# Turning the attention weights and the head outputs of six heads on VectorE instead of TensorE

## What is computed

```python
def diff_attention(h, w_qkv, w_out, ...):      # 8 heads, two maps each, value width 256
    proj = h @ w_qkv
    # q, k: (S, 8, 2, 128), v: (S, 8, 256)
    logits = einsum('bqhcd,bkhcd->bhcqk', qb, k) * scale
    p = softmax(logits + bias, axis=-1)
    a = p[:, :, 0] - lam * p[:, :, 1]          # the attention weights
    o = einsum('bhqk,bkhe->bqhe', a, v)
    o = rmsnorm(o, subln_g) * (1 - lambda_init) # the normed head output
    return o.reshape(B, S, 8 * 256) @ w_out
```

## Time and profile before

| | us |
|---|---|
| median of 3 runs | 2162.86 (2162.79 to 2163.11) |
| span of the profiled execution, first to last instruction | 2161.1 |
| TensorE matmuls busy | 2152.5 |
| VectorE busy | 1394.3 |
| ScalarE busy | 1020.2 |
| GpSimd busy | 15.1 |

### The profile page before, as it was taken

One profiled execution on the slowest core, in us unless ns is written; L12 is line 12 of the kernel. 1 busy time (PEld: TensorE's weight loads), 2 busy tenths in 40 slices (PEclk: granted clock), 3 DMA queues, 4 the chain that ended last, 5 costly groups with the idle time before them and its releaser, 6 DMA issues.

```text
span 2161.1 us, 30888 instructions
## 1 busy us (share of the span) xinstructions
PE 2152.5 (100%) x11158; PEld 1836.9 (85%) x11158; DVE 1394.3 (65%) x1951; ACT 1020.2 (47%) x1430; POOL 15.1 (1%) x28
## 2 busy tenths in 40 slices
PE   9999999999999999999999999999999999999998
PEld 8888888888888888888888888888888888888887
DVE  7777756755764665675577777657646656755754
ACT  6444445443543443454445445455434434434543
POOL 1000000000000000000000000000000000000000
PEclk9999999999999999999999999999999999999999
DMA  9644456555555555555555544545555555555553
GB/s 331 230 176 157 165 185 214 195 195 185 187 194 193 194 188 191 186 192 188 182 176 175 176 163 169 195 177 193 194 194 179 192 193 195 185 195 186 192 194 117
DMA packets 63567, 408.92 MB, mean 189 GB/s; under 512 B 6677, under 2 KB 12565, under 8 KB 15482
## 3 DMA queue, kind: packets, MB, share of 16 engines
q1 hardware_dynamic: 60304, 402.42, 52.2%
q10 hardware_dynamic: 2730, 3.55, 0.5%
q0 software_dynamic: 448, 1.77, 0.2%
HBM read 405.58 MB, written 2.14 MB: 189 GB/s over the span
## 4 chain that ended last, share of the span: by engine, by line
PE 99%; issue 0%; DVE 0%; POOL 0%; POOLq 0%; DVEq 0%; ACT 0%
PE acc L1093 32%; PE acc L1097 16%; PE ps_scores L1127 7%; PE ps_scores L1125 7%; PE ps_scores L1126 7%; PE ps_v L1125 4%; PE ps_v L1126 4%; PE ps_v L1127 4%; PE acc L1125 2%; PE acc L1126 2%; PE acc L1127 2%; PE ps_aux L1126 2%; PE ps_aux L1125 2%; PE ps_aux L1127 2%; PE ps_scores L1184 1%; PE ps_o L1184 1%
## 5 line engine op out<-in xcount | busy, mean ns | idle before, releaser
L666 DVE TENSOR_TENSOR w_lo<-raw,w_hi 128x1024 fp32r<-128x1024 f32 x744 | 908.6, 1223 | 513.9 <-ACT w_hi L362 511.4
L362 ACT ACTIVATE w_hi<-raw 128x1024 fp32r<-128x1024 f32 x744 | 787.4, 1059 | 632.4 <-PE ps_scores L1127 253.4
L1093 PE MATMUL acc<-gx,w_hi 128*128 128x512 f32 x3008 | 947.4, 396 | 0.0
L1097 PEld LDWEIGHTS acc<-gx,w_lo 128*128 128x128 f32 x3008 | 565.0, 188 | 133.4
L1097 PE MATMUL acc<-gx,w_lo 128*128 128x256 f32 x3008 | 591.5, 278 | 0.0
L1093 PEld LDWEIGHTS acc<-gx,w_hi 128*128 128x128 f32 x3008 | 460.3, 189 | 2.6 <-issue 0.5
L1125 PE MATMUL ps_scores<-w_hi,mid 128*128 128x512 f32 x640 | 249.5, 390 | 0.0
L1127 PE MATMUL ps_scores<-w_hi,mid 128*128 128x512 f32 x640 | 249.0, 389 | 0.0
L1126 PE MATMUL ps_scores<-w_lo,mid 128*128 128x512 f32 x640 | 249.0, 389 | 0.0
L369 ACT ACTIVATE copied<-acc 128x256 f32<-128x256 f32 x188 | 71.8, 382 | 317.4 <-PE acc L1097 317.4
L699 DVE TENSOR_TENSOR head<-acc,copied 128x256 f32<-128x256 f32 x188 | 79.8, 424 | 176.4 <-ACT copied L369 175.0
(11 more groups left out here) (201 smaller groups left out, 1629.1 us busy)
## 6 DMA issues: line engine op xcount, KB each, us to landing
raw<-weights_dram SPq DMA_DIRECT2D x372, 1024.0 KB, 4.8
raw<-opening_dram SPq DMA_DIRECT2D x5, 512.0 KB, 8.4
bias<-bias_line SPq DMA_DIRECT2D x2, 1024.0 KB, 10.4
x<-x_tok_dram SPq DMA_DIRECT2D x2, 1024.0 KB, 12.1
bias<-bias_line ACTq DMA_DIRECT2D x2, 1024.0 KB, 8.4
raw<-opening_dram SPq DMA_DIRECT2D x5, 256.0 KB, 5.7
bias<-x_fm_dram SPq DMA_DIRECT2D x5, 256.0 KB, 8.5
bias<-bias_line SPq DMA_DIRECT2D x2, 512.0 KB, 13.0
```

What stands on the lines that cost most here:

```text
L362: act.activation(w_hi[:, n % RING, :], raw[:, u % RAW_SLOTS, part * HALF:(part + 1) * HALF], ACT.Copy).then_inc(hi_ready, 1)
L666: dve.tensor_tensor(w_lo[:, n % RING, :], raw[:, u % RAW_SLOTS, part * HALF:(part + 1) * HALF], w_hi[:, n % RING, :].bitcast(F32), ALU.sub ...
L1093: pe.matmul(acc[w % 2][:], w_hi[:, n % RING, j * P:(j + 1) * P], gx[:, kt, :], start=kt == 0, stop=False)
L1097: ins = pe.matmul(acc[w % 2][:, SEQ:], w_lo[:, n % RING, i * P:(i + 1) * P], gx[:, kts[i], 0:SEQ], start=False, stop=kts[i] == KT - 1)
```

## The change

For heads 0 to 5 (`by_vector`) the eight TensorE transposes of a head fall away. VectorE turns 32x32 blocks in their place: `turn_blocks` issues one instruction for each pair of a row group i and a column group j of 32, each over the 2 x 2 blocks of that kind in the 256 x 256 matrix, 16 for `attn` and 16 for `o_norm`. Their result is written to SBUF, into a slot of the bias tile that is free in this layer (`turned_head`), from which `copy_attn`, `lo_attn`, `hi_att1` and `lo_att1` read. The 16 are issued in two halves, `UPPER` around one split and `LOWER` behind the next: those of `attn` in unit u + 5, those of `o_norm` in unit u + 1 of the next head, ahead of and behind the evacuation and the second split. `copy_attn` and `lo_attn` move from the end of u + 5 into the first half of the next head's unit u; `hi_att1` moves from the end of u + 1 to behind `exps` in u + 2, ahead of `copy_cross`, and `lo_att1` to the end of u + 2. Heads 6 and 7 are turned on TensorE as before.

```diff
+QUAD = 32
+QUADS = P // QUAD
+        turned_head = bias[:, A_HEADS - 1, :, :]
+        turned_head_blocks = turned_head.rearrange("p a (t i r) -> p t a i r", t=QT, i=QUADS)
...
             def copy_attn(n):
                 def step():
-                    act.wait_ge(pt_ready, n + 1)
+                    if by_vector(n):
+                        act.wait_ge(attn_turned, QUADS * (n - A_HEADS + 1))
+                    else:
+                        act.wait_ge(pt_ready, pe_turns(n))
                     act.wait_ge(o_ready, n)
-                    act.activation(attn_t[:, 0, :, :], ps_attn_t[:, :, ::-1], ACT.Copy).then_inc(pt_copied, 1)
+                    act.activation(attn_t[:, 0, :, :], attn_source(n)[:, :, ::-1], ACT.Copy).then_inc(pt_copied, 1)
...
                 elif not lean_before:
-                    narrow(u, w)
+                    narrow(u, w, first=[copy_attn(n - 1)])
                     last_values = C_HEADS // V_HEADS1 - 1
-                    narrow(u + 1, w + 1, before=[o_squares(h - 1)], second=[hi_att1(h - 1)] +
-                           ([values_hi(1, last_values, 3 + last_values)] if h == LEAN1 else []))
+                    narrow(u + 1, w + 1, before=[o_squares(h - 1)],
+                           second=[values_hi(1, last_values, 3 + last_values)] if h == LEAN1 else [])
...
-                narrow(u + 2, w + 2, first=[exps(0, s, n)])
+                turned_last = [hi_att1(h - 1)] if h and not lean_before else []
+                narrow(u + 2, w + 2, first=[exps(0, s, n)] + turned_last)
...
-                    quarter(u + 5, second=[copy_attn(n)] + ([values_hi(1, group_v, 3 + group_v)] if now else []))
+                    quarter(u + 5, second=[values_hi(1, group_v, 3 + group_v)] if now else [])
...
+            def turn_blocks(source, rows, signal):
+
+                for i in rows:
+                    for j in range(QUADS):
+                        ins = dve.transpose(turned_head_blocks[j * QUAD:(j + 1) * QUAD, :, :, i, :],
+                                            source[i * QUAD:(i + 1) * QUAD, :, :, j, :])
+                    ins.then_inc(signal, 1)
+
+            attn_blocks = attn[:].rearrange("p t (a j c) -> p t a j c", a=QT, j=QUADS)
+            norm_blocks = o_norm.rearrange("p t (a j c) -> p t a j c", a=2, j=QUADS)
+
+            def turn_attn(h, rows):
+                def step():
+                    dve.wait_ge(attn_ready, QT * (A_HEADS + h + 1))
+                    if h:
+                        dve.wait_ge(mid_ready, MID_ATT1 + 2 * h)
+                    turn_blocks(attn_blocks, rows, attn_turned)
+                return step
+
+            def turn_output(h, rows):
+                def step():
+                    dve.wait_ge(onorm_ready, QT * (h + 1))
+                    dve.wait_ge(pt_split, A_HEADS + h + 1)
+                    turn_blocks(norm_blocks, rows, output_turned)
+                return step
+
+            UPPER, LOWER = range(QUADS // 2), range(QUADS // 2, QUADS)
...
                 elif not lean_before:
-                    narrow(u, w, to_qa)
+                    narrow(u, w, to_qa, first=[lo_attn(A_HEADS + h - 1)])
                     last_values = C_HEADS // V_HEADS1 - 1
-                    narrow(u + 1, w + 1, to_ka, before=[head_norm(h - 1)], second=[lo_att1(h - 1)] +
+                    narrow(u + 1, w + 1, to_ka, before=[head_norm(h - 1)], first=[turn_output(h - 1, UPPER)],
+                           second=[turn_output(h - 1, LOWER)] +
                            ([values_lo(1, last_values, 3 + last_values)] if h == LEAN1 else []))
...
-                narrow(u + 2, w + 2, to_qb, first=[scores1(0, h)])
+                turned_last = [lo_att1(h - 1)] if h and not lean_before else []
+                narrow(u + 2, w + 2, to_qb, first=[scores1(0, h)], second=turned_last)
...
-                    quarter(u + 5, second=[lo_attn(A_HEADS + h)] +
+                    quarter(u + 5, first=[turn_attn(h, UPPER)], second=[turn_attn(h, LOWER)] +
                             ([values_lo(1, group_v, 3 + group_v)] if last and h < LEAN1 - 1 else []))
...
-                    narrow(u + 1, w + 1, hooks=({}, {8: [turn_output(h - 1)]}))
+                    narrow(u + 1, w + 1)
...
-                    values1(group_v, u + 5, part + 1, late=[turn_attn(A_HEADS + h)])
+                    values1(group_v, u + 5, part + 1)
```

More of the change, by code:

```diff
@@ L228, in trunk @@
         x_done, turned = sem("x_done"), sem("turned")
+        attn_turned, output_turned = sem("attn_turned"), sem("output_turned")
         x_folded, sums_ready = sem("x_folded"), sem("sums_ready")
@@ L267, in store_rows, with by_vector, pe_turns, attn_source @@
             eng.dma_start(out.rearrange("(t p) d -> p t d", p=P)[:, t, lo:hi], y[:, t, lo:hi]).then_inc(y_stored, 16)
+        def by_vector(n):
+            return A_HEADS <= n < A_HEADS + LEAN1
+        def pe_turns(n):
+            return n + 1 if n < A_HEADS else n - LEAN1 + 1
+        def attn_source(n):
+            return turned_head if by_vector(n) else ps_attn_t
+        def output_source(h, j):
+            return turned_head[:, j, :] if h < LEAN1 else attn_flat[:, j * SEQ:(j + 1) * SEQ]
         def columns(g):
@@ L603, in step @@
                 def step():
-                    act.wait_ge(ot_ready, h + 1)
+                    if h < LEAN1:
+                        act.wait_ge(output_turned, QUADS * (h + 1))
+                    else:
+                        act.wait_ge(ot_ready, h - LEAN1 + 1)
                     for j in range(2):
-                        act.activation(mid[:, 2 * h + j, 0:SEQ], attn_flat[:, j * SEQ:(j + 1) * SEQ], ACT.Copy,
+                        act.activation(mid[:, 2 * h + j, 0:SEQ], output_source(h, j), ACT.Copy,
                                        scale=sub_gain[:, j:j + 1]).then_inc(mid_hi, 1)
@@ L803, in step @@
                     dve.wait_ge(pt_copied, n + 1)
-                    dve.tensor_tensor(attn_t[:, 1, :, :], ps_attn_t[:, :, ::-1], attn_t[:, 0, :, :].bitcast(F32),
+                    dve.tensor_tensor(attn_t[:, 1, :, :], attn_source(n)[:, :, ::-1], attn_t[:, 0, :, :].bitcast(F32),
                                       ALU.subtract).then_inc(pt_split, 1)
@@ L972, in step @@
                     dve.wait_ge(soft_steps, n + 4)
-                    dve.wait_ge(pt_ready, A_HEADS + h)
+                    if h <= LEAN1:
+                        dve.wait_ge(pt_ready, A_HEADS)
+                        dve.wait_ge(attn_turned, QUADS * h)
+                    else:
+                        dve.wait_ge(pt_ready, pe_turns(A_HEADS + h - 1))
                     for t in range(QT):
@@ L985, in step @@
                     dve.wait_ge(oinv_ready, h + 1)
-                    if h:
-                        dve.wait_ge(ot_ready, h)
+                    if 0 < h <= LEAN1:
+                        dve.wait_ge(output_turned, QUADS * h)
+                    elif h:
+                        dve.wait_ge(ot_ready, h - LEAN1)
                     for t in range(QT):
@@ L997, in step @@
                         t = 2 * h + j
-                        dve.scalar_tensor_tensor(mid[:, t, SEQ:], attn_flat[:, j * SEQ:(j + 1) * SEQ],
+                        dve.scalar_tensor_tensor(mid[:, t, SEQ:], output_source(h, j),
                                                  sub_gain[:, j:j + 1], mid[:, t, 0:SEQ].bitcast(F32),
@@ L1204, in step @@
                         pe.wait_ge(map_copied, 1)
-                    elif n <= A_HEADS:
+                    elif n < A_HEADS:
                         pe.wait_ge(pt_split, n)
```

## The result

The changed kernel takes 2217.69 us (2217.48 to 2218.57) against 2162.85 us for the kernel before: 54.8 us slower, ratio 1.0255 with a 95% interval of 1.0242 to 1.0268. The forecast was 2202.3, the range 2180 to 2224. The profiled execution spans 2215.7 us.

A forecast was written before the change was run, and what follows sets the result against it. TensorE was taken to bound the kernel. Six heads late by 5.91 us each, net of the transposes removed, make 35.5 us; value splits add 3.9, so 2162.9 + 39.4 = 2202.3 us, range 2180 to 2224.

The forecast's parts named there:

- What bounds the kernel: TensorE, busy 2152.5 of 2161.1 us at full clock with one 1.1 us wait, sets the time if operands come in time.
- What is removed: Two groups of four TensorE transposes a head, 0.44 us each, in heads 0 to 5: 5.3 us in all.
- D: Time from one VectorE transpose's start to the next: 0.31 us, every one of the 192 held by changing partitions.
- The copies from SBUF: Copies and subtractions reading the transposed result from SBUF in place of PSUM: costed at nothing.
- Place (a): Product with the values, end of a head's first unit: late by 16D - 2.22, 2.74 us, waiting for `lo_attn`.
- Place (b): Scores of the first map, middle of the third unit: late by 8D - 1.43, 1.05 us.
- Place (c): Scores of the second map, middle of the fifth unit: late by 8D + 0.52, 3.00 us.
- The value split at (a): `values_lo`, 1.31 us ahead of `lo_attn` after heads 1 and 3; with head 6's at Place (c), 3.9 us.
- The sum of the queue: Lateness less what is given back, 32D - 4.01 a head, six times 35.5 us, plus 3.9: 39.4 us.
- the clock: Rival: TensorE works at 1.2 GHz for as long as it waited, about 20 us more, 2223; chance 0.10.
- the rival "faster": All added work falls into VectorE's 8 to 10 idle us a head, gaining 5.3 us, 2157.6; chance 0.03.
- dearer transposes: Rival: an element costs twice, D = 0.42, 60.5 us, 2223.4; chance 0.08 with D above 0.36.

The follow-up runs named there:

- spread: Kernel before, with only the outputs of heads 0 to 4 turned on VectorE, in five pieces laid in its idle times: 2160.24 us against 2162.43.
- same_rows: Changed kernel, each transpose writing the 32 partitions it reads, four in a row in the same group, blocks landing in the wrong place: 2190.64 us.
- by_columns: Changed kernel with the two loops of the block transpositions exchanged, so the group written stays for four instructions and the one read changes: 2218.99 us.
- attn_only: Changed kernel with only the attention weights of heads 0 to 5 turned on VectorE, the outputs left on TensorE: 2192.71 us.
- filled: Changed kernel with throwaway 128 x 512 matmuls on TensorE ahead of the two long waits of a head: 2206.12 us, ratio 1.020.
- out_only: Changed kernel with only the normed outputs of heads 0 to 5 turned on VectorE, the attention weights left on TensorE: 2196.53 us.

## Why the prediction was right, and where it fell short

- What bounds the kernel: right. TensorE never waited before, and what came late was paid.
- What is removed: right. `spread` gives back 2.2 us for five groups, 0.44 each.
- D, the price of a transpose: right in size (0.319 for the 0.31 taken) and in its reason, shown by `same_rows` and `by_columns`, but for the "every one of the 192": the first of each upper eight, 12 in all, isn't held.
- The copies from SBUF, put at nothing: right for VectorE, `lo_attn` takes 0.68 us as before; ScalarE's take up to 0.05 us longer (L633 494 ns for 470, `copy_attn` 630 for 583), too little to show in the sum.
- Place (a), head 0's product: 2.74 worked out, 3.05 measured; with D = 0.319 it is 2.88, and the rest is 0.12 us that the second eight wait for the end of the split ahead of them (1119.70 to 1120.96 is 1.26 us, not 1.14) and the way from VectorE's result to TensorE's start (1124.68 + 0.68 = 1125.36, and 1125.51). The later heads wait less there, 2.41 us, or 3.73 with the value split; in `attn_only`, where nothing is late at (c), it is 3.05 throughout, so the steps were added up as if they didn't bear on each other. Place (b): 1.05 against 1.05. Place (c): 3.00 against 2.96. That these two agree so well is in part luck: start to start, which is what was worked out, TensorE is late by 11.06 - 9.79 = 1.27 us at (b) and 15.05 - 11.83 = 3.22 at (c) (head 5, 1321.24 to 1336.29), more than the idle time that the profile lists, and the formula with D = 0.319 gives 1.12 and 3.07. The value split at (a): 1.31 against 3.73 - 2.41 = 1.32; but at head 6 its 1.31 us went into a wait of 1.12 us for the bank of the next unit (L1157), and not into (c) itself, which is 2.84.
- The sum of the queue: 39.4 us forecast, 41.1 with the measured D, 41.3 as 54.8 less the clock's 13.5, about 41.8 by `filled`.
- Two slips that moved nothing: the operand at (c) stands 0.45 us ahead of its use in the kernel before (1145.38 less 1144.93), not 0.6; and in the rival "faster" 8D + 0.52 is over zero for any D, so by the prediction's own steps the whole 5.3 us could never be had.
- The step that failed is the clock. The sum has no term for it: it stood among the rivals with a chance of 0.10 and a price of 20 us, as something that might happen besides, and it is part of the likeliest case. It cost about 13.5 of the 15.4 us by which the forecast missed; the other 2 are the queue's share. The trace before, which shows no dip, shows no wait of 2 us either, so it could say nothing. The range reached to 2224 because of this rival and of dearer transposes (2223.4), which didn't come; the forecast of 2202.3 by itself wasn't met.

## What to carry to other kernels

Work moved off the bounding engine isn't free because the other engine is idle a quarter of the time: find, for each operand that the bounding engine takes from it, how far ahead it is finished now (here 2.5, 1.0 and 0.5 us), and add the new instructions to the ones in front of it. Work cut into pieces as long as the idle times that the time line shows cost nothing here (one 256 x 256 a head, five heads); twice as much a head in blocks of eight cost 42.7 us of waits for a gain of 5.3. And where a full TensorE queue gets new waits of 2 us and more, put the clock behind them into the sum as well as the wait; here it was a quarter of the loss.

## What the runs showed of the hardware

- TensorE's granted clock went to half for about 3.4 us behind waits in a queue that otherwise ran at 2.4 GHz, for 6.8 us in six cases, three of them at waits over 4 us. Over the seven kernels that wait, no wait up to 1.6 us had that with it, 5 of 16 waits of 2.0 to 2.4 us did, and 34 of 37 of 2.8 us and more (not the changed kernel's first, 3.05 us, one of 2.97 in `out_only` and one of 3.72 in `by_columns`). What decides in the other cases stays open. Price: 1.6 us for 3.4, since 512-column matmuls start 0.43 us apart in place of 0.23.
- VectorE's 32 x 128 float32 transpose takes 0.19 us from start to start while it stays in its partitions (`same_rows`) and 0.315 us where it changes them each time, read or written (0.319 with what follows the eight).
- Turning 256 x 256 costs TensorE 0.44 us in its stream and VectorE 16 x 0.319 = 5.1 us.
